# Weight blocks of a fused two-layer transformer block: units taken one after the other, matmuls of one width in runs, and unrolled gate and up bodies

## The chip, the cores and the metric

The kernel runs on one core of one Trainium2 chip. The metric is the device time of one execution in microseconds, here as the median of several runs; smaller is better. One further execution was profiled, and all rows of the trace come from it.

## What is computed

The reference takes one sequence of 256 tokens with 2048 channels through two transformer blocks in float32 (shapes and names cut to what matters here):

```
first_block:   h = norm(x); x += nsa_attention(h) @ w_out          # kv, q, cv, misc, vb, wo
               h = norm(x); x += relu(h @ ffn_w1)**2 @ ffn_w2      # ff0..ff3, fd0..fd3 (8192 hidden)
               h = norm(x); x += sigmoid(h @ ple_w_gate) * (p @ ple_w_proj)   # proj, gate
               x = norm_final(x)
second_block:  h = norm(x); m = swa_sink_attention(h) @ w_out      # k2, v2, q2, wo2
               x += norm(m)
               h = norm(x); u = conv3(h @ ffn_w_up)                # up0..up2 (5632 gates, 5632 values)
               x += norm((silu(u_gate) * u_value) @ ffn_w_down)    # dn0..dn2
```

Nearly all of the work is the product of a weight matrix with 256 columns of activations.

## The kernel before

**Layout.** Activations are kept transposed: a tile is 128 channels by 256 tokens. Each activation operand (A for the inputs of projections, H for hidden tiles) is held as a hi part, rounded to fp32r, and a lo part, the rest, side by side: `A[:, k, :, :]` is 512 columns, hi then lo. A weight block is 128 x 128. Its product with a tile is made of hi x hi, hi x lo (one matmul of 512 columns with the hi weights, line 370) and lo x hi (one matmul of 256 columns with the lo weights, line 367). The two halves of the 512-column PSUM bank are added later.

**Weights.** The host lays all weights out as a stream of 757 pieces of 512 KB, each of 8 blocks (BLK). A ring of 4 slots (SLOTS) holds them. For each piece SyncE issues the DMA (line 319), when the lo half of the piece four before it is done; ACT casts it to the hi half (`split_hi`, line 1101), when TensorE has used the slot; DVE subtracts to get the lo half (`split_lo`, line 655); TensorE waits for `lo_ready`, multiplies, and raises `piece_used` after the last matmul of the piece.

**Units and stages.** A unit is one 128-row output tile, that is K blocks (K = 16, in dn2 12, in proj 2) summed in one of four PSUM banks. A stage is a run of units with the same operand: kv, q, wo, each ff and fd, gate, q2, wo2, dn0 and dn1 have 16 units (32 pieces), k2 has 4, up0 and up1 have 32 (64 pieces), up2 has 24 (48), dn2 has 16 of 12 blocks (24). They go through `units` (line 339), called in loops of four units (`Fori`) with eight pieces each. cv, v2 and vb use other code (`compress`, `natural`, lines 498 and 394): 512-column matmuls with activations as the stationary operand, in cv in turn with runs of eight 256-column ones (line 506). proj uses the `narrow` branch of `units` (lines 359 to 361): three 256-column matmuls for each block.

**The order of the blocks** is `order` (line 104), for the host's stream and for TensorE alike. Where K is over 8 and at most 16, four units go together: blocks k = 0..3 of each of the four, then k = 4..7 of each, then the rest of each:

```python
return [(j, k) for g in range(0, n, 4) for a, b in ((0, 4), (4, 8), (8, K)) for j in range(g, g + 4) for k in range(a, b)]
```

So the four units of a group end in its last four pieces, one piece apart. Within a block the hi matmul comes first and then the lo one, in a unit's last block the other way round.

**What follows a unit.** DVE walks through the pieces in `body` (line 657). At each step it splits the piece that is LEAD + 2 = 5 ahead of the one just done, then runs `late` for the units that ended `lag` pieces ago, and then empties the bank of the units that ended in this piece: `tensor_reduce` (line 691) adds the two halves into one of four z tiles and raises `z_ready`. TensorE's next unit in the same bank waits for that (line 351). ACT's `body` (line 1108) is alike, with `each` one piece and `late` two pieces after a unit's end. POOL takes z (`take`, line 1385), mostly by a multiplication with the norm factor rs (line 1391).

In the gate stage the chain of a unit is: reduce (DVE), times rs (POOL, line 1460), sigmoid (ACT), times the proj tile and added to x (POOL, 1462 and 1464), next operand's hi and two squares (ACT, 1291 to 1293), its lo and a sum of squares (DVE, 979 to 984), another sum (POOL, 1467). In the up stages it is: reduce (DVE), times rs into ub (POOL, 1500), first tap (ACT, 1345), second and third tap (DVE, `conv`, 1046 and 1049), and for each pair of a gate and a value unit a sigmoid (ACT, 1351), two products (POOL, 1504 and 1510), a cast into H (ACT, 1354) and its lo half (POOL, 1516). up0 begins behind a norm, so its first two groups are handled by one body of eight units, in which the first four are held back four pieces (`hold`, line 1068). All these bodies are loops over groups of four units on DVE, ACT and POOL.

Of the kernel before, what the change touches and what calls it, by code (L numbers as in the profile page):

```python
# [74 lines left out]
NZ = {"cv": 0, "vb": 0, "v2": 0, "misc": 1, "proj": 0, "wo2": 0, "dn0": 0, "dn2": 0}  # L75
# [28 lines left out]
def order(n, K):  # L104

    if not 8 < K <= 16:  # L110
        return [(j, k) for j in range(n) for k in range(K)]
    return [(j, k) for g in range(0, n, 4) for a, b in ((0, 4), (4, 8), (8, K)) for j in range(g, g + 4) for k in range(a, b)]


def ends(n, K):

    at = {}
    for b, (j, k) in enumerate(order(n, K)):
        if k == K - 1:
            at.setdefault(b // BLK, []).append(j)  # L120
    return at
# [19 lines left out]
def program(nc, xT, pT, wstream, consts, setup, params, out):  # L141
# [11 lines left out]
    with ExitStack() as ctx:  # L153
# [182 lines left out]
        def _(pe):  # L336
            pe.sem_inc(piece_used, SLOTS)

            def units(p, p0, u, u0, n, K, moving, ready=None, between={}, narrow=False):

                for b, (j, k) in enumerate(order(n, K)):
                    s = (p0 + b // BLK) % SLOTS
                    if b % BLK == 0:
                        pe.wait_ge(lo_ready, p + (b // BLK + 1))
                    if k == 0:  # L350
                        pe.wait_ge(z_ready, u + (j - 3 if narrow and j >= 4 else j + 1))
                    if ready and j == 0:
                        pe.wait_ge(*ready(k))
                    bank = psum[(u0 + j) % 4 + (j // 4 % 2 * 4 if narrow else 0)]
                    w = slice(b % BLK * P, b % BLK * P + P)
                    m = moving(j, k)

                    if narrow:
                        nc.tensor.matmul(bank[:, 0:S], whi[:, s, w], m[:, 0, :], start=(k == 0), stop=False)
                        nc.tensor.matmul(bank[:, 0:S], whi[:, s, w], m[:, 1, :], start=False, stop=False)  # L360
                        last = nc.tensor.matmul(bank[:, 0:S], wlo[:, s, w], m[:, 0, :], start=False, stop=(k == K - 1))
                        if b % BLK == BLK - 1:
                            last.then_inc(piece_used, 1)
                        continue

                    def lo():
                        return nc.tensor.matmul(bank[:, 0:S], wlo[:, s, w], m[:, 0, :], start=False, stop=False)  # L367
                    if k == K - 1:
                        lo()
                    last = nc.tensor.matmul(bank[:, :], whi[:, s, w], m, start=(k == 0), stop=(k == K - 1))  # L370
                    if k < K - 1:
                        last = lo()
                    if b % BLK == BLK - 1:
                        last.then_inc(piece_used, 1)
                        if b // BLK in between:
                            between[b // BLK]()
# [112 lines left out]
            project("kv", 0, between={NORM_AT["kv"]: lambda: norm("kv")})  # L489
# [82 lines left out]
            with pe.Fori(0, 4) as it:  # L572
                units(it * 8 + PB["wo"], PB["wo"], it * 4 + UB["wo"], UB["wo"], 4, DT, lambda j, k: H[:, k, :, :],
                      lambda k: (att["nsa"]["o_ready"], k // HPG * 2 + 2))
# [7 lines left out]
            def chunk(c, first=0):  # L582
# [3 lines left out]
                with pe.Fori(0, 4) as it:  # L586
                    units(o * 64 + it * 8 + PB[fd], PB[fd], o * 32 + it * 4 + UB[fd], UB[fd], 4, CH,
                          lambda j, k: H[:, k, :, :], lambda k: (ff_ready, c * CH + (k + 1)))
            hidden(0, 0, between={NORM_AT["ff0"]: lambda: norm("ff0")})
# [5 lines left out]
            units(PB["proj"], PB["proj"], UB["proj"], UB["proj"], DT, 2, lambda j, k: pA[:, k, :, :], narrow=True)  # L595
# [11 lines left out]
            def norms_k2():  # L607
# [3 lines left out]
                  between={NORM_AT["k2"]: norms_k2})  # L611
# [7 lines left out]
            with pe.Fori(0, 4) as it:  # L619
                units(it * 8 + PB["wo2"], PB["wo2"], it * 4 + UB["wo2"], UB["wo2"], 4, DT, lambda j, k: H[:, k, :, :],  # L620
                      lambda k: (att["swa"]["o_ready"], k // HPG * 2 + 2))
# [4 lines left out]
            for c, n in enumerate(CHUNKS2):  # L626
# [5 lines left out]
                if c == 0:  # L632
                    hidden2(0, between={NORM_AT["up0"]: lambda: norm("up0", parts=(acc[:, :], acc2))})
                with pe.Fori(1 if c == 0 else 0, n // 2) as it:
                    hidden2(it)
                if n == CH:
                    with pe.Fori(0, 4) as it:
                        units(it * 8 + PB[dn], PB[dn], it * 4 + UB[dn], UB[dn], 4, n, lambda j, k: H[:, k, :, :],
                              lambda k: (up_ready, t0 + k + 1))
                else:  # L640
                    for it in range(2):
                        units(it * n + PB[dn], PB[dn], it * 8 + UB[dn], UB[dn], 8, n, lambda j, k: H[:, k, :, :],
                              lambda k: (up_ready, t0 + k + 1))
# [5 lines left out]
        def _(dve):  # L649
# [7 lines left out]
            def body(p, p0, u, u0, zu, z0, n, K, late=None, lag=1, skip=0, short=0, between={}, dst=None, narrow=False, add=False,  # L657
                     hold=0):

                at = ends(n, K)
                count = n * K // BLK
                for q in range(LEAD, count + AHEAD):
# [11 lines left out]
                    for j in at.get(q - LEAD, []):  # L679
                        dve.wait_ge(piece_used, p + (SLOTS + q - LEAD + 1))  # L680
# [959 lines left out]
```

## Time and profile before

| | us |
|---|---|
| median of 3 runs | 2458.48 (2455.64 to 2459.03) |
| the profiled execution | 2456.7 |
| its span, first to last instruction | 2454.9 |
| TensorE busy | 2312.4 (94%) |
| DVE busy | 1580.3 (64%) |
| ACT busy | 1095.4 (45%) |
| POOL busy | 768.8 (31%) |

In the trace's names PE is TensorE's matmuls, PEld its weight loads, and L691 line 691 of the kernel. A matmul's own length includes its way through the array and overlaps the next one, so the pace of TensorE is read from the distance of starts, not from lengths. PEclk is the granted TensorE clock as a share of full speed. Some matmul records can be missing, so counts of matmuls in a window are a little low. The sums of the prediction are made against the profiled execution.

### The profile page before, as it was taken

The page shows a single profiled execution, that of the slowest core. Times are in us where ns is not written, and L with a number is a line of the kernel's source. Part 1 is how long each engine was busy: PE and PEld are TensorE (multiplying, and loading weights), DVE is VectorE, ACT ScalarE, POOL GpSimd, SP SyncE. Part 2 cuts the span into 40 slices and gives each one's busy share as a digit, 9 for nine tenths or more (in the row PEclk, how much of TensorE's full clock was granted, in tenths as well). Part 3 has the DMA queues.
Part 4 walks back from the last instruction along what each step waited for, and adds up shares of the span by engine and source line. Part 5 has one row for each costly group of instructions (what it writes and reads, how often), then busy time and mean ns, then how long its engine had stood idle before and what let it go on. Part 6 is the DMA issues. An engine that isn't in the chain of part 4 may idle for free.

```text
span 2454.9 us, 39475 instructions
## 1 busy us (share of the span) xinstructions
PE 2312.4 (94%) x12668; PEld 1970.6 (80%) x12668; DVE 1580.3 (64%) x2021; ACT 1095.4 (45%) x1635; POOL 768.8 (31%) x755
## 2 busy tenths in 40 slices
PE   8999899999999999999999988978999989999996
PEld 7888668888888888888877866867788878888885
DVE  7676666666666666656666785586665566666666
ACT  5334444543443443454553354454443444434442
POOL 4111004441441441344561200244440244413443
PEclk9999899999999999999999989989999999999998
DMA  6556115555555555555545521534445544554552
GB/s 238 171 198 209 61 39 180 183 187 187 180 194 187 174 195 187 180 188 177 175 161 197 183 100 62 186 112 161 155 165 194 176 158 168 169 184 164 178 171 96
DMA packets 115118, 407.04 MB, mean 166 GB/s; under 512 B 12464, under 2 KB 16848, under 8 KB 115056
## 3 DMA queue, kind: packets, MB, share of 16 engines
q1 hardware_dynamic: 110592, 401.64, 48.4%
q10 hardware_dynamic: 4464, 4.61, 0.6%
q8 instruction: 35, 0.57, 0.1%
q14 instruction: 27, 0.22, 0.0%
HBM read 404.05 MB, written 2.15 MB: 165 GB/s over the span
## 4 chain that ended last, share of the span: by engine, by line
PE 60%; issue 20%; DVE 8%; POOL 7%; ACT 3%; POOLq 0%; DMA 0%; ACTq 0%; DVEq 0%; SPq 0%
PE bank L370 35%; PE bank L367 18%; POOL PT L1391 2%; POOL bias L1510 2%; DVE wboth L655 1%; PE bank L457 1%; PE bank L407 1%; PE bank L462 1%; PE bank L408 1%; PE bank L409 1%; POOL x L1464 1%; DVE Sm L1046 1%; ACT Sm L1156 1%; POOL Sm L1504 1%; PE bank L430 1%
## 5 line engine op out<-in xcount | busy, mean ns | idle before, releaser
L655 DVE TENSOR_TENSOR wboth<-raw,wboth 128x1024 fp32r<-128x1024 f32 x757 | 993.8, 1321 | 513.3 <-ACT wboth L1101 509.5
L370 PE MATMUL bank<-A,wboth 128*128 128x512 f32 x3200 | 1141.0, 405 | 57.8 <-DVE z L691 41.7
L1101 ACT CAST wboth<-raw 128x1024 fp32r<-128x1024 f32 x757 | 784.8, 1046 | 727.3 <-PE bank L370 325.7
L370 PE MATMUL bank<-H,wboth 128*128 128x512 f32 x2560 | 897.8, 400 | 8.8 <-DVE z L691 8.8
L367 PE MATMUL bank<-A,wboth 128*128 128x256 f32 x3200 | 876.1, 284 | 1.4 <-DVE A L735 1.4
L370 PEld LDWEIGHTS bank<-A,wboth 128*128 128x128 f32 x3200 | 599.7, 191 | 200.6 <-DVE z L691 49.5
L367 PE MATMUL bank<-H,wboth 128*128 128x256 f32 x2560 | 694.9, 282 | 0.0
L367 PEld LDWEIGHTS bank<-A,wboth 128*128 128x128 f32 x3200 | 616.2, 193 | 19.7 <-DVE A L735 1.7
L370 PEld LDWEIGHTS bank<-H,wboth 128*128 128x128 f32 x2560 | 473.4, 189 | 113.4 <-DVE z L691 10.1
L367 PEld LDWEIGHTS bank<-H,wboth 128*128 128x128 f32 x2560 | 486.6, 190 | 15.5 <-issue 0.5
L691 DVE TENSOR_REDUCE z<-bank 128x256 f32<-128x512 f32 x316 | 217.1, 687 | 55.2 <-PE bank L370 47.4
L1391 POOL TENSOR_TENSOR PT<-z,rs 128x256 f32<-128x256 f32 x88 | 131.8, 1498 | 350.2 <-DVE z L691 349.9
L1419 POOL TENSOR_TENSOR x<-x,z 128x256 f32 x80 | 79.0, 987 | 409.7 <-DVE z L691 409.7
L1391 POOL TENSOR_TENSOR bias<-z,rs 128x256 f32<-128x256 f32 x80 | 109.3, 1366 | 170.2 <-DVE z L691 170.2
L1383 POOL TENSOR_TENSOR acc<-acc,bias 128x256 f32<-128x256 f32 x80 | 79.8, 998 | 238.0 <-ACT bias L1320 152.4
L1046 DVE SCALAR_TENSOR_TENSOR Sm<-PT,par 128x256 f32<-128x256 f32 x88 | 51.5, 585 | 127.5 <-ACT PT L1345 127.5
L1345 ACT ACTIVATE PT<-PT,par 128x256 f32<-128x256 f32 x88 | 44.7, 508 | 117.7 <-POOL PT L1391 117.7
L1391 POOL TENSOR_TENSOR y<-z,Sm 128x256 f32 x32 | 37.9, 1183 | 167.0 <-DVE z L691 167.0
L1354 ACT CAST H<-bias 128x256 f32 (+1 forms) x44 | 17.9, 406 | 130.9 <-POOL bias L1510 130.9
L1259 ACT ACTIVATE Sm<-bias 128x256 f32<-128x256 f32 x64 | 26.8, 418 | 103.1 <-POOL bias L1391 103.1
L1156 ACT ACTIVATE Sm<-Sm,small 128x256 f32<-128x256 f32 (+1 forms) x128 | 56.5, 445 | 19.4 <-DVE small L761 13.1
L430 PE MATMUL bank<-kT,y 64*128 64x128 f32 (+3 forms) x256 | 51.5, 377 | 10.3 <-DVE bias L944 7.2
(196 smaller groups left out, 1394.8 us busy)
## 6 DMA issues: line engine op xcount, KB each, us to landing
raw<-wstream SPq DMA_DIRECT2D x757, 512.0 KB, 3.3
bias<-bias_rows ACTq DMA_DIRECT2D x8, 512.0 KB, 3.4
x<-xT SPq DMA_DIRECT2D x4, 512.0 KB, 6.9
out<-x SPq DMA_DIRECT2D x3, 512.0 KB, 2.7
out<-x SPq DMA_DIRECT2D x2, 256.0 KB, 2.0
Sm<-pT ACTq DMA_DIRECT2D x1, 256.0 KB, 2.7
con<-consts SPq DMA_DIRECT2D x1, 254.0 KB, 9.9
par<-params SPq DMA_DIRECT2D x1, 244.0 KB, 3.2
```

Of the source, the lines that this page charges most:

```text
L367: return nc.tensor.matmul(bank[:, 0:S], wlo[:, s, w], m[:, 0, :], start=False, stop=False)
L370: last = nc.tensor.matmul(bank[:, :], whi[:, s, w], m, start=(k == 0), stop=(k == K - 1))
L430: last = nc.tensor.matmul(bank, lhs, rhs, start=True, stop=True)
L655: V.tensor_tensor(wlo[:, s, :], raw[:, s, :], whi[:, s, :].bitcast(F32), ALU.subtract).then_inc(lo_ready, 1)
L691: V.tensor_reduce(dst(j) if dst else z[:, (z0 + j) % 4, :], psum[(u0 + j) % 4][:, :].rearrange("p (h c) -> p c h", h=2), AX, ALU.add).then ...
L1046: V.scalar_tensor_tensor(tA[:, slot, :], ub[:, slot, 1:S + 1], w[1], c0[:, slot % 2, :], ALU.mult, ALU.add).then_inc(up_step, 1)
L1101: C.copy(whi[:, s, :], raw[:, s, :]).then_inc(hi_ready, 1)
L1156: last = C.activation(probs[:, e - e0, :], probs[:, e - e0, :], ACT.Exp, bias=nmx[:, i:i + 1], accum_out=sums[:, i:i + 1])
L1383: G.tensor_tensor(dst, dst, src, ALU.add).then_inc(acc_step, 1)
L1391: return lambda zz: G.tensor_tensor(dst, zz, by, ALU.mult)
L1419: lambda zz: G.tensor_tensor(tile(x, it * 4 + j), tile(x, it * 4 + j), zz, ALU.add))
L1510: G.tensor_tensor(zr[:, j, :], tC[:, j - 1, :], tB[:, j, :], ALU.mult).then_inc(up_h, 1)
```

## The change

The order changes: all K blocks of a unit come one after the other, except in the first `mixed` groups of a stage, which keep the old order (the first group of kv, wo, ff0, each fd, gate, k2, wo2, dn0 and dn1, the first two of up0, all of dn2). In `units` a piece is done as eight hi matmuls and eight lo ones instead of eight pairs; pieces with a unit's first block begin with hi, those with its last block with lo, so that two neighbouring pieces join runs of the same width. In the gate stage each block becomes three 256-column matmuls into half a bank (`narrow`), DVE multiplies that half by rs straight into zr (`gate_in`) instead of reducing into z, and POOL's multiplication goes; the next operand of a unit is made three pieces after its end instead of two. TensorE's first iteration of wo, fd, wo2, dn0 and dn1 is written out ahead of the loop. The bodies of DVE, ACT and POOL for gate and up are written out over all units instead of looping over four; POOL's order in up and gate changes with it (below).

```diff
-def order(n, K):
...
+def order(n, K, mixed=0):
+
+    out = []
+    for g in range(0, n, 4):
+        js = range(g, min(g + 4, n))
+        cuts = ((0, 4), (4, 8), (8, K)) if g // 4 < mixed else ((0, K),)
+        out += [(j, k) for a, b in cuts for j in js for k in range(a, b)]
+    return out
...
+                    def his():
+                        for i, (j, k) in enumerate(piece):
+                            if his_first:
+                                arrive(j, k)
+                            last = nc.tensor.matmul(bank(j)[:, :], whi[:, s, cols(i)], moving(j, k), start=(k == 0), stop=(k == K - 1))
+                        return last
+
+                    def los():
+                        for i, (j, k) in enumerate(piece):
+                            if not his_first:
+                                arrive(j, k)
+                            last = nc.tensor.matmul(bank(j)[:, 0:S], wlo[:, s, cols(i)], moving(j, k)[:, 0, :], start=False, stop=False)
+                        return last
...
+                        ks = [k for _, k in piece]
+                        his_first = 0 in ks or (K - 1 not in ks and q % 2 == 1)
+                        if his_first:
+                            his()
+                            last = los()
+                        else:
+                            los()
+                            last = his()
+                    last.then_inc(piece_used, 1)
...
-                      lambda k: (a2_ready, k + 1), **more)
-            gate(0, between={NORM_AT["gate"]: lambda: norm("gate")})
+                      lambda k: (a2_ready, k + 1), narrow=True, **more)
+            gate(0, mixed=1, between={NORM_AT["gate"]: lambda: norm("gate")})
...
-                for q in range(LEAD, count + AHEAD):
+                for q in range(LEAD, count + max(AHEAD, LEAD + lag)):
...
+                        if direct:
+                            direct(j).then_inc(z_ready, 1)
+                            continue
...
+            def gate_in(j):
+
+                if j == 0:
+                    dve.wait_ge(rs_ready, 4)
+                if j >= 4:
+                    dve.wait_ge(ple_sig, j - 3)
+                return V.tensor_tensor(zr[:, j % 4, :], psum[(UB["gate"] + j) % 4][:, 0:S], rs[:, :], ALU.mult)
             dve.wait_ge(acc_zero, 3)
-            gate(0, between={NORM_AT["gate"]: lambda: norm(rs[:, :], 3).then_inc(rs_ready, 1)})
-            with dve.Fori(1, 4) as it:
-                gate(it)
+            body(PB["gate"], PB["gate"], UB["gate"], UB["gate"], ZB["gate"], ZB["gate"], DT, DT, next_lo, lag=3, mixed=1, direct=gate_in,
+                 between={NORM_AT["gate"]: lambda: norm(rs[:, :], 3).then_inc(rs_ready, 1)})
...
+                def hidden2(**more):
+                    body(PB[up], PB[up], UB[up], UB[up], ZB[up], ZB[up], 2 * n, DT, lambda j: conv(2 * t0 + j, j % 4), **more)
...
+            body(PB["gate"], PB["gate"], 0, DT, DT, sigmoid, next_input, lag=3, mixed=1,
+                 between={NORM_AT["gate"]: lambda: root(3, rs[:, :])})
...
-            with pool.Fori(0, 4) as it:
-                for j in range(4):
-                    t = it * 4 + j
-                    take(it * 4 + UB["gate"], ZB["gate"], j, mul(zr[:, j, :], rs[:, :]))
+            for t in range(DT + 2):
+                if t < DT:
                     pool.wait_ge(ple_sig, t + 1)
...
+                for i in range(n):
+                    preact(2 * i)
+                    if i:
+                        product_lo(i - 1)
+                    preact(2 * i + 1)
+                    gated(i)
+                    product(i)
+                product_lo(n - 1)
```

POOL's order for two pairs of units in up was: preact 0, preact 1, gated 0, preact 2, product 1, preact 3, product_lo 1, gated 2, product 3, product_lo 3.

## Rows read from the trace of the kernel before

**Rows 1.** Page: span, and busy time of each engine.

```profile
span 2454.9 us, 39475 instructions
PE 2312.4 (94%) x12668; PEld 1970.6 (80%) x12668; DVE 1580.3 (64%) x2021; ACT 1095.4 (45%) x1635; POOL 768.8 (31%) x755
```

**Rows 2.** Windows at stage borders: us, length, busy (count) by engine, clock, DMA.

```profile
533.40:984.60 451.20, 451.20 (x2561) 392.29 (x2560) 279.44 (x241) 192.79 (x228) 132.91 (x149) 1.00 0.55 186
1177.90:1279.30 101.40, 94.61 (x515) 81.25 (x515) 64.37 (x81) 54.17 (x91) 59.74 (x58) 0.97 0.49 165
1279.30:1333.90 54.60, 48.87 (x232) 40.53 (x231) 35.41 (x45) 23.21 (x31) 18.21 (x16) 0.94 0.46 156
1667.10:1822.30 155.20, 141.68 (x769) 121.41 (x768) 99.14 (x124) 70.07 (x100) 70.44 (x62) 0.96 0.48 164
1822.30:1916.80 94.50, 91.92 (x513) 79.69 (x513) 54.72 (x56) 35.98 (x38) 7.76 (x7) 0.98 0.55 182
1916.80:2116.00 199.20, 186.26 (x1026) 160.50 (x1025) 124.37 (x153) 88.66 (x123) 82.77 (x73) 0.97 0.49 166
2210.90:2359.00 148.10, 139.29 (x769) 119.97 (x768) 92.93 (x113) 66.28 (x91) 60.83 (x54) 0.98 0.49 167
```

**Rows 3.** Waits: who waited for whom, total us, times, longest.

```profile
PE bank L370 <- DVE z L691: 50.5, 26, 2.9
```

**Rows 4.** Timeline, end of up1: start us, length, engine, line, what.

```profile
2112.76 0.68 DVE L691 TENSOR_REDUCE z<-bank 128x256 f32<-128x512 f32 x1
...
2113.52 1.66 POOL L1391 TENSOR_TENSOR PT<-z,rs 128x256 f32<-128x256 f32 x1 [2.63 <-DVE z L691]
...
2115.32 0.51 ACT L1345 ACTIVATE PT<-PT,par 128x256 f32<-128x256 f32 x1 [2.03 <-POOL PT L1391]
...
2115.98 0.48 DVE L1046 SCALAR_TENSOR_TENSOR Sm<-PT,par 128x256 f32<-128x256 f32 x1 [1.41 <-ACT PT L1345]
...
2117.02 0.68 DVE L691 TENSOR_REDUCE z<-bank 128x256 f32<-128x512 f32 x1
...
2122.26 0.69 DVE L691 TENSOR_REDUCE z<-bank 128x256 f32<-128x512 f32 x1
```

**Rows 5.** Windows: 3 us behind the wait in dn1.

```profile
2124.00:2127.00 3.00, 3.00 (x11) 2.52 (x10) 1.46 (x4) 1.44 (x2) 2.05 (x3) 0.50 0.50 175
```

**Rows 6.** Timeline in ff3: the first and tenth 512-column matmul.

```profile
1007.00 0.40 PE L370 MATMUL bank<-A,wboth 128*128 128x512 f32 x1
...
1010.18 0.40 PE L370 MATMUL bank<-A,wboth 128*128 128x512 f32 x1
```

**Rows 7.** Timeline in wo: the first and 21st 512-column matmul.

```profile
353.02 0.40 PE L370 MATMUL bank<-H,wboth 128*128 128x512 f32 x1
...
359.96 0.40 PE L370 MATMUL bank<-H,wboth 128*128 128x512 f32 x1
```

**Rows 8.** Timeline in v2: the first and 55th 512-column matmul.

```profile
1317.62 0.39 PE L408 MATMUL bank<-wboth,H 128*128 128x512 f32 x1
...
1329.87 0.39 PE L408 MATMUL bank<-wboth,H 128*128 128x512 f32 x1
```

**Rows 9.** Timeline in proj: the first and 47th 256-column matmul.

```profile
984.64 0.28 PE L359 MATMUL bank<-pA,wboth 128*128 128x256 f32 x1
...
990.16 0.29 PE L360 MATMUL bank<-pA,wboth 128*128 128x256 f32 x1
```

**Rows 10.** Timeline in cv: the starts of two periods.

```profile
205.63 0.40 PE L407 MATMUL bank<-wboth,A 128*128 128x512 f32 x1
...
209.33 0.40 PE L407 MATMUL bank<-wboth,A 128*128 128x512 f32 x1
```

**Rows 11.** Groups by line, splits: busy us, mean ns | idle before.

```profile
L655 DVE TENSOR_TENSOR wboth<-raw,wboth 128x1024 fp32r<-128x1024 f32 x757 | 993.8, 1321 | 513.3 <-ACT wboth L1101 509.5
...
L1101 ACT CAST wboth<-raw 128x1024 fp32r<-128x1024 f32 x757 | 784.8, 1046 | 727.3 <-PE bank L370 325.7
```

**Rows 12.** Groups by line: weight loads of the lo matmuls.

```profile
L367 PEld LDWEIGHTS bank<-A,wboth 128*128 128x128 f32 x3200 | 616.2, 193 | 19.7 <-DVE A L735 1.7
```

More of the change, by code:

```diff
@@ L73 @@
 PB, UB, ZB = {}, {}, {}
-NZ = {"cv": 0, "vb": 0, "v2": 0, "misc": 1, "proj": 0, "wo2": 0, "dn0": 0, "dn2": 0}
+NZ = {"gate": 0, "cv": 0, "vb": 0, "v2": 0, "misc": 1, "proj": 0, "wo2": 0, "dn0": 0, "dn2": 0}
 _p = _u = _z = 0
@@ L101, with ends @@
                     ("g3", DT), ("conv", 3 * 2 * FF2_T), ("pos_k", CL), ("pos_v", CL), ("sink", SWA_HEADS)])
-def order(n, K):
[L110 to L115, printed above, removed]
+def order(n, K, mixed=0):
[5 more added lines that the diff above has]
+    return out
+def ends(n, K, mixed=0):
     at = {}
-    for b, (j, k) in enumerate(order(n, K)):
+    for b, (j, k) in enumerate(order(n, K, mixed)):
         if k == K - 1:
@@ L337, in _ @@
             pe.sem_inc(piece_used, SLOTS)
[L339 to L356, printed above, removed]
-                    if narrow:
[L359 to L376, printed above, removed]
@@ new lines, in units, with bank, arrive, cols @@
+            def units(p, p0, u, u0, n, K, moving, ready=None, between={}, narrow=False, banks=4, mixed=0):
+                blocks = order(n, K, mixed)
+                for q in range(len(blocks) // BLK):
+                    piece = blocks[q * BLK:q * BLK + BLK]
+                    s = (p0 + q) % SLOTS
+                    pe.wait_ge(lo_ready, p + (q + 1))
+                    def bank(j):
+                        return psum[(u0 + j) % 4 + (j // 4 % 2 * 4 if banks == 8 else 0)]
+                    def arrive(j, k):
+                        if k == 0:
+                            pe.wait_ge(z_ready, u + (j - 3 if banks == 8 and j >= 4 else j + 1))
+                        if ready and j == 0:
+                            pe.wait_ge(*ready(k))
+                    def cols(i):
+                        return slice(i * P, i * P + P)
+                    def his():
[10 more added lines that the diff above has]
+                        return last
+                    if narrow:
+                        for i, (j, k) in enumerate(piece):
+                            arrive(j, k)
+                            m = moving(j, k)
+                            nc.tensor.matmul(bank(j)[:, 0:S], whi[:, s, cols(i)], m[:, 0, :], start=(k == 0), stop=False)
+                            nc.tensor.matmul(bank(j)[:, 0:S], whi[:, s, cols(i)], m[:, 1, :], start=False, stop=False)
+                            last = nc.tensor.matmul(bank(j)[:, 0:S], wlo[:, s, cols(i)], m[:, 0, :], start=False, stop=(k == K - 1))
+                    else:
[4 more added lines that the diff above has]
+                            last = los()
+                        else:
+                            los()
+                            last = his()
+                    last.then_inc(piece_used, 1)
+                    if q in between:
+                        between[q]()
@@ L1120, in body @@
                         between[q - LEAD - 1]()
-                    for step, lag in ((late, 2), (each, 1)):
+                    for step, behind in ((late, lag), (each, 1)):
                         if step:
-                            for j in at.get(q - LEAD - lag - hold, []):
+                            for j in at.get(q - LEAD - behind - hold, []):
                                 if hold == 0 or j < 4:
                                     step(j)
-                            for j in at.get(q - LEAD - lag, []):
+                            for j in at.get(q - LEAD - behind, []):
                                 if hold and j >= 4:
```

268 lines of the change are left out of this document (135 added, 133 removed).

## The prediction

> **What bounds the kernel now.** I read the engine shares first: TensorE is busy for 94% of the 2454.9 us span, no other engine for more than 64% [rows 1]. So the question is what the remaining waits of TensorE are, and how fast it goes where it does not wait. The windows cut at the stage borders (where the matmuls of TensorE turn from operand A to operand H and back) answer both [rows 2]. From fd0 to fd2 there are 5 x 32 = 160 pieces of eight weight blocks in 451.2 us, with TensorE busy all the time: 2.82 us a piece, TensorE-bound. In up1 the same work, 64 pieces, takes 199.2 us instead of 180.5; the last 48 pieces of up0 take 155.2 and the 48 of up2 148.1 instead of 135.4; dn0 94.5, gate 101.4 instead of 90.2. The waits name the cause: 26 waits of the 512-column matmul, 50.5 us, for the DVE reduce that empties a bank [rows 3]. There is one near each border of a group of four units, in up, dn, gate and k2 alone.
>
> Why the reduce is late is seen in the timeline at the end of up1 [rows 4]. Reduce (0.68), POOL's scaling (1.66), ACT's tap (0.51), two convolution steps on DVE, and only then the next reduce, 4.26 us after the first; the last one comes 5.24 us later, because ACT first waited for POOL's product. The old order ends the four units of a group one piece (2.82 us) apart, and DVE handles a unit's convolution one piece after its end, ahead of the next reduce. So DVE falls behind by 1.4 us or more with each unit of the burst, and the bank of the fourth is empty too late. After the longer waits the clock costs extra: in the 3 us behind such a wait at the start of dn1 the granted clock is half [rows 5], 1.2 GHz instead of 2.4.
>
> **The width of the matmuls.** A block is a 512-column matmul with the hi weights and a 256-column one with the lo weights, and the old order alternates them. Nine such pairs in steady state take 3.18 us, 353.3 ns each [rows 6]. Twenty pairs just after the wait at wo take 6.94 us, 347.0 ns [rows 7]; this lasts some four pieces after a wait, then 353 returns. The trace also has runs of one width: 54 steps of 512 columns in v2 take 12.25 us, 226.9 ns each [rows 8]; 46 steps of 256 columns in proj take 5.52 us, 120.0 ns each [rows 9], directly behind 450 us of the 353 pace. Together 346.9: a run of each width costs 6.4 ns a block less than the alternation.
>
> [...]
>
> **The change, part by part.** *Runs of one width* (units). A piece becomes 8 x 226.9 + 8 x 120.0 = 2.775 us. A change of width remains once in two pieces each way; cv has such a period, 12 of 512 and 8 of 256 columns in 3.70 us [rows 10], against 12 x 0.2269 + 8 x 0.120 = 3.683, so 0.017 for both changes and 2.784 a piece. I take 2.78. The bounds are 2.775 and the old 2.82. Of the 720 pieces with pairs, gate's 32 leave. 416 lie in quiet stages (kv, q, wo, ff, fd, q2, wo2); about 16 of these already run at the quick pace, so 400 x 0.040 = 16.0 us.
>
> *Units in sequence.* Units now end two pieces (5.56 us) apart; only the first group of a stage whose operand is still being made keeps the old order. A bank is wanted again six pieces after its unit ends. At the full pace up1 would take 64 x 2.78 = 177.9 (21.3 less), up2 133.4 (14.7 less), the 48 pieces of up0 133.4 (21.8 less), dn0 89.0 (5.5 less; dn1 and dn2 repeat its waits, so 16.5 for three). That is 74.3 us. What stays: DVE per unit needs the chain of 4.26, in which one split of a piece fits, and a second split of 1.22 to 1.32 [rows 4, 11], so 5.48 to 5.58 against 5.56 of TensorE. It just fits. A lag does not stop TensorE at once: a slot freed by piece p takes 1.05 for ACT's cast and 1.3 for DVE [rows 11], and is wanted 3 x 2.78 = 8.3 us later, a slack of 6.0 us. I leave 5 us in up0, whose first eight units still come in bursts and hand on a backlog, 1.5 at the start of each dn and 2.5 for the cycle: 12 us, bounds 0 and 39 (second rival). So 62.3 us.
>
> *Gate.* Three runs of 256 columns are 24 x 120.0 = 2.88 us a piece, 92.2 for 32, dearer than 2.78. DVE's multiply out of the half bank replaces its reduce and POOL's scaling. No row has this multiply; it reads half the columns of the reduce (0.68), so I bound it by 0 and 0.68, take no cost, and DVE's per-unit work stays under the 5.76 us of two pieces. The multiply adds a wait on DVE, for the norm and from unit 4 on for ACT's sigmoid of the unit four before; behind it DVE has the next split, and TensorE waits for that. The norm was ahead of the reduce before, and that unit ended eight pieces ago, so 0. ACT's next input and DVE's lo of it move one piece back; for the last unit they stand behind a split that needs k2's first piece used, 2.8 us late, and k2 wants them in its fifth piece, 11 us on: 0. With the waits gone and 1 us left for the norm: 101.4 - 93.2 = 8.2 us.
>
> *k2 and v2* take 54.6 us [rows 2]. TensorE's norm sums wait there for POOL's additions and v2 for the norm chain. Gate's last unit no longer queues behind three others, so I take off 4 us (bounds 0 and 8: the second is about what exceeds 16 pieces).
>
> *Unrolled bodies* of DVE, ACT and POOL: the arithmetic per unit is the same, only register steps go and more code is fetched; TensorE's loops remain. Cover: the 6 us of slack above; I set 0, bounds -1 and +3. The weight DMAs are the same 757, drawn 1.5% faster at a DMA share of 0.55 in fd [rows 2], so 0. The extra TensorE bodies for first groups and the host's reordering cost nothing during the run, under the same cover. Attention, the start and the last norm are untouched.
>
> Sum: 16.0 + 62.3 + 8.2 + 4 = 90.5. The profiled execution took 2456.7 us (1.8 around its span), and the median of the runs shown is 2458.48, 1.8 above it. So 2366.2 for the former and **2368 us** for the median, 3.7% faster.
>
> **Rivals.** *First: the order of widths is not the cause.* The same alternation runs at 347.0 after a wait and 353.3 later, so something that builds up over four pieces may build up in runs too. Against it: 12 us of 512 and 5.5 us of 256 without it [rows 8, 9]. Then the 648 pieces in the sum (400, the 160 of up and the 88 of dn) keep 2.82, 25.9 us more: 2394. Chance 0.14. [...]
>
> *Second: DVE's chain paces the up bodies.* If every second unit keeps the 5.24 us step, the cycle averages 4.75 + 1.22 = 5.97, 0.41 over two pieces; over 88 units 36 us, less up to 18 for the slack of three stages: 18 to 36, say 27 more, 2395. For it: the fit within 0.1 us. Against: POOL now issues the product straight behind the convolution, so ACT's wait that made 5.24 goes. Chance 0.14.
>
> *Third, the other side: weight loads show in the run of lo matmuls.* Each 256-column matmul needs its own 128x128 load, and a load is 193 ns long in the trace [rows 12]; in the alternation each second load hides under 512 columns. In 648 pieces there are 5184 lo matmuls; the 90.5 us are gone when each takes 17 ns above 120, and at 193 the time would be 2368 + 5184 x 0.073 = 2746. The decision lies at 137 ns. Against it: proj and cv run 256 columns at 120 with as many loads as matmuls [rows 1, 9, 10]. Chance 0.03. A further 0.03 is for rivals one and two together with a cost that no row shows, which ends near no change.
>
> **How the numbers follow.** Forecast 0.66, rivals as given. The likeliest case alone spans 2351 (no residue, 2.775, 2 us more at gate and k2) to 2382. For 8 in 10 I take 2349 to 2394, up to rivals one and two, about half of which is inside. Measurement can tell about 0.2%, 5 us, from no change: faster 0.66 + 0.14 + 0.14 = 0.94, same 0.03, slower 0.03.
>
> **What would show it.** In the profile after: fd stages at 2.775 to 2.785 us a piece, with 227 and 120 ns inside a run; waits of the hi matmul for the reduce down from 26 to fewer than eight; up1 within 178 to 182 us; gate 92 to 94; no half-clock stretch in the up stages after the first 16 pieces. A pace of 2.82 in fd proves the first rival; a calm fd with up1 above 185 proves the second; lo steps above 130 ns the third. The forecast is wrong if fd does not move or if TensorE waits for weight splits in up.

## The result, and the profile after

The changed kernel takes 2362.6 us (median of four runs, 2358.8 to 2363.4) against 2457.1 for the kernel before on the same chip: a ratio of 0.9616, interval 0.9597 to 0.9635. The forecast was 2368, 3.7% faster; it is 3.8%. The profiled execution took 2362.7 us, its span 2360.8.

The page of the kernel after, span and engine busy times [rows 1]:

```profile
span 2360.8 us, 38219 instructions
PE 2265.9 (96%) x12924; PEld 1971.3 (83%) x12924; DVE 1631.3 (69%) x2021; ACT 1104.6 (47%) x1635; POOL 725.7 (31%) x739
```

The span fell by 94 us and TensorE's busy time by 46.5: so half of the gain is idle time gone, and half is busy time saved by matmuls that run faster, at the quicker pace or at full clock. The windows of the kernel after at the stage borders show where (columns as in [rows 2]; the stretches are ff2 with fd2, gate, k2 with v2, up0's last 48 pieces, dn0, up1, up2):

```profile
798.80:977.00 178.20, 178.20 (x1027) 157.45 (x1026) 117.54 (x96) 80.69 (x96) 51.75 (x64) 1.00 0.56 188
1167.70:1260.30 92.60, 92.60 (x771) 92.52 (x771) 73.40 (x85) 57.81 (x96) 50.56 (x48) 1.00 0.57 188
1260.30:1309.60 49.30, 47.06 (x231) 39.72 (x230) 34.07 (x41) 21.23 (x26) 11.37 (x10) 0.97 0.52 171
1642.30:1780.00 137.70, 134.88 (x769) 118.04 (x769) 105.80 (x130) 73.11 (x104) 71.69 (x66) 1.00 0.56 189
1780.00:1869.10 89.10, 89.10 (x514) 78.69 (x513) 51.79 (x50) 34.43 (x34) 4.82 (x4) 1.00 0.56 191
1869.10:2047.30 178.20, 178.20 (x1026) 157.48 (x1025) 144.29 (x159) 94.31 (x126) 83.37 (x76) 1.00 0.55 188
2136.40:2270.00 133.60, 133.60 (x769) 118.07 (x768) 107.65 (x118) 70.38 (x94) 62.03 (x57) 1.00 0.55 188
```

In up1 TensorE is now busy without a gap, at full clock, for the 178.2 us that 64 quiet pieces take in ff2 and fd2. Up1 became 21 us shorter: 12.9 of it were idle (199.20 less 186.26 busy), 2.3 are the new pace (64 x 0.036), and the remaining 5.8 fit the matmuls at half clock behind the waits (the mean clock of the window rose from 0.97 to 1.00).

The waits of the kernel after, TensorE's rows for the reduce (now line 716), for weight splits (685) and for A's blocks (760); line 362 is now the wide (512-column) matmul and 369 the narrow (256-column) one:

```profile
PE bank L362 <- DVE A L760: 9.1, 4, 7.8
PE bank L362 <- DVE wboth L685: 5.4, 3, 3.9
PE bank L369 <- DVE wboth L685: 4.9, 5, 1.5
PE bank L369 <- DVE A L760: 3.5, 3, 1.6
PE bank L362 <- DVE z L716: 0.3, 1, 0.3
```

The 50.5 us for reduces [rows 3] have become 0.3. Four of the waits for splits, 2.7 us together, lie in the last 48 pieces of up0; up1, dn0 and up2 have none. The timeline of TensorE in up1 shows the runs:

```profile
1894.95 3.82 PE L362 MATMUL bank<-A,wboth 128*128 128x512 f32 x16
1898.61 2.08 PE L369 MATMUL bank<-A,wboth 128*128 128x256 f32 x16
1900.52 3.82 PE L362 MATMUL bank<-A,wboth 128*128 128x512 f32 x16
```

Start to start, sixteen wide matmuls take 3.66 us (228.8 ns each) and sixteen narrow ones 1.91 (119.4 ns): 5.57 us for two pieces, 2.785 a piece. The other engines' timeline in the same place, to be read against [rows 4]:

```profile
1906.07 0.48 DVE L1086 SCALAR_TENSOR_TENSOR Sm<-PT,par,Sm 128x256 f32<-128x256 f32 x1
...
1906.63 1.65 POOL L1549 TENSOR_TENSOR bias<-Sm 128x256 f32<-128x256 f32 x1 [0.88 <-DVE Sm L1086]
...
1908.13 0.69 DVE L716 TENSOR_REDUCE z<-bank 128x256 f32<-128x512 f32 x1 [0.43 <-PE bank L362]
1908.32 0.41 ACT L1394 CAST H<-bias 128x256 fp32r<-128x256 f32 x1 [1.88 <-POOL bias L1549]
...
1913.70 0.69 DVE L716 TENSOR_REDUCE z<-bank 128x256 f32<-128x512 f32 x1 [0.23 <-PE bank L362]
```

Now DVE waits for TensorE (0.43 and 0.23 us at a reduce), not TensorE for DVE; the reduces are 5.57 us apart, two pieces. POOL's product starts 0.08 us behind the convolution (1906.07 + 0.48).

One stretch became worse. Timeline of TensorE at the start of up0 after:

```profile
1601.35 0.38 PE L369 MATMUL bank<-A,wboth 128*128 128x256 f32 x1 [1.43 <-DVE A L760]
1602.22 0.78 PE L369 MATMUL bank<-A,wboth 128*128 128x256 f32 x2 [0.49 <-DVE A L760]
1604.62 0.58 PE L369 MATMUL bank<-A,wboth 128*128 128x256 f32 x1 [1.62 <-DVE A L760]
```

The run of narrow matmuls waits for each block of A as DVE makes it, and the eight wide ones, which could have filled some of these waits, all come behind. The fifth piece takes 9.16 us, before 5.05; from wo2's last matmul to the end of the sixteenth piece it is 70.0 us, before 69.0.

### The profile page after: what moved, and what is told of

The parts are those of the page before. It is cut to its first block, busy times and chain, and to the rows that moved or that the text cites. A ratio compares the mean times of both kernels' runs of the same rounds, so it can differ in the third digit from the quotient of the medians.

```text
span 2360.8 us, 38219 instructions
## 1 busy us (share of the span) xinstructions
PE 2265.9 (96%) x12924; PEld 1971.3 (83%) x12924; DVE 1631.3 (69%) x2021; ACT 1104.6 (47%) x1635; POOL 725.7 (31%) x739
## 4 chain that ended last, share of the span: by engine, by line
PE 85%; DVE 7%; ACT 3%; POOL 3%; issue 2%; DMA 0%; POOLq 0%; SPq 0%; ACTq 0%; DVEq 0%
PE bank L362 48%; PE bank L369 25%; PE bank L376 1%; PE bank L378 1%; PE bank L377 1%; PE bank L471 1%; PE bank L476 1%; POOL bias L1431 1%; DVE wboth L685 1%; PE bank L421 1%; PE bank L423 1%; PE bank L422 1%; ACT Sm L1192 1%; DVE Sm L782 1%; ACT wboth L1141 1%
## 5 line engine op out<-in xcount | busy, mean ns | idle before, releaser
L362 PE MATMUL bank<-A,wboth 128*128 128x512 f32 x2944 | 713.2, 393 | 15.0 <-DVE A L760 9.1
L362 PEld LDWEIGHTS bank<-A,wboth 128*128 128x128 f32 x2944 | 543.4, 190 | 124.2 <-issue 15.6
L362 PE MATMUL bank<-H,wboth 128*128 128x512 f32 x2560 | 617.8, 391 | 0.3 <-DVE z L716 0.3
L362 PEld LDWEIGHTS bank<-H,wboth 128*128 128x128 f32 x2560 | 468.9, 188 | 91.3 <-issue 1.0
L369 PEld LDWEIGHTS bank<-A,wboth 128*128 128x128 f32 x2944 | 381.0, 192 | 26.7 <-DVE wboth L685 6.3
L369 PE MATMUL bank<-A,wboth 128*128 128x256 f32 x2944 | 388.0, 284 | 9.1 <-DVE wboth L685 4.9
L369 PEld LDWEIGHTS bank<-H,wboth 128*128 128x128 f32 x2560 | 331.2, 191 | 14.3
L369 PE MATMUL bank<-H,wboth 128*128 128x256 f32 x2560 | 335.8, 283 | 0.0
L1431 POOL TENSOR_TENSOR PT<-z,rs 128x256 f32<-128x256 f32 x88 | 75.0, 853 | 280.8 <-DVE z L716 280.1
L1431 POOL TENSOR_TENSOR bias<-z,rs 128x256 f32<-128x256 f32 x64 | 61.1, 955 | 160.0 <-DVE z L716 160.0
L1549 POOL TENSOR_TENSOR bias<-Sm 128x256 f32<-128x256 f32 x44 | 70.1, 1592 | 39.5 <-DVE Sm L1086 39.5
L376 PE MATMUL bank<-A,wboth 128*128 128x256 f32 x256 | 72.6, 284 | 0.0
L377 PE MATMUL bank<-A,wboth 128*128 128x256 f32 x256 | 72.4, 283 | 0.0
L378 PE MATMUL bank<-A,wboth 128*128 128x256 f32 x256 | 72.4, 283 | 0.0
L1477 POOL TENSOR_TENSOR Sm<-Sm 128x256 f32<-128x256 f32 x64 | 59.4, 927 | 33.8 <-ACT Sm L1299 33.8
```

The source lines that it names most:

```text
L362: last = nc.tensor.matmul(bank(j)[:, :], whi[:, s, cols(i)], moving(j, k), start=(k == 0), stop=(k == K - 1))
L369: last = nc.tensor.matmul(bank(j)[:, 0:S], wlo[:, s, cols(i)], moving(j, k)[:, 0, :], start=False, stop=False)
L376: nc.tensor.matmul(bank(j)[:, 0:S], whi[:, s, cols(i)], m[:, 0, :], start=(k == 0), stop=False)
L377: nc.tensor.matmul(bank(j)[:, 0:S], whi[:, s, cols(i)], m[:, 1, :], start=False, stop=False)
L378: last = nc.tensor.matmul(bank(j)[:, 0:S], wlo[:, s, cols(i)], m[:, 0, :], start=False, stop=(k == K - 1))
L1431: return lambda zz: G.tensor_tensor(dst, zz, by, ALU.mult)
```

## Experiments

After the result my theory was that of the prediction: pace by runs, waits gone by the sequence of units. The rivals were that POOL's new order or the unrolled bodies had removed the waits, and for the pace, that something other than the order of widths sets it. Every run is set against the kernel before on its chip. "Up and dn" is the time from wo2's last matmul to dn2's last in the profiled execution, one of each kernel (before 832.8 us, after 764.6).

**Pairs again**, in the changed kernel's units:

```diff
-                        if his_first:
-                            his()
-                            last = los()
...
+                        for i, (j, k) in enumerate(piece):
+                            arrive(j, k)
+                            for half in ((1, 0) if k == K - 1 else (0, 1)):
...
```

> The changed kernel with one thing undone: in every piece the eight blocks are done as pairs again, hi (512 columns) then lo (256), in a unit's last block lo then hi. Units stay in sequence, gate and the unrolled bodies stay. Theory (alternating widths is what made a piece 2.82 us): fd, ff and up1 pieces go back from 2.784 to 2.82 us, so 656 pieces x 0.036 = 24 us more, less about 5 us at the stages that start on an operand still being made, where a pair can follow each arrival: about 2381 us, up1 near 180.5. Rival (the pace came from the order of the units, or from waits that are gone): pieces stay at 2.784 and the time at 2357 to 2363 us.

2385.7 us, ratio 0.9716 (0.9700 to 0.9732): the runs are worth 23 to 25 us (by the medians, and by the ratios). The window of the same two stages, ff2 and fd2, in this kernel:

```profile
808.00:988.50 180.50, 180.50 (x1037) 157.20 (x1036) 116.52 (x97) 80.69 (x96) 52.09 (x65) 1.00 0.53 185
```

2.82 us a piece, as before: undoing the order of widths, and nothing else, brings the old pace back.

**Runs alone**: the kernel before, with the changed kernel's units and nothing else (old order of units, loops, gate).

> The kernel before with the runs of one width alone: same order of units in groups of four, same loops, same gate with 512 + 256 columns; only a piece is done as eight hi and eight lo matmuls. Theory (the two parts are independent, and the sequence is worth about 70 us by itself): quiet pieces at 2.784 to 2.79, the 26 waits for the reduce stay, up1 stays at 196 to 199 us since there DVE's burst sets the pace; 583 pieces x 0.036 = 21 us less, some 5 us given back at stage starts: 2438 to 2446 us. Rival one (runs only pay with units in sequence): 2457. Rival two (runs also relieve the bursts): under 2425.

2442.4 us, ratio 0.9951 (0.9935 to 0.9968), as expected. Its waits:

```profile
PE bank L363 <- DVE z L706: 53.7, 28, 3.3
```

In up and dn only 6.9 us are gained (825.9): a faster matmul there mostly waits longer.

**POOL's old order** in the changed kernel's unrolled up bodies:

```diff
-                for i in range(n):
+                for i in range(0, n, 2):
                     preact(2 * i)
-                    if i:
-                        product_lo(i - 1)
                     preact(2 * i + 1)
                     gated(i)
+                    preact(2 * i + 2)
                     product(i)
-                product_lo(n - 1)
+                    preact(2 * i + 3)
+                    product_lo(i)
+                    gated(i + 1)
...
```

> The changed kernel with POOL's order in the up stages as before the change (the product of a pair of units stands behind the scaling of the next unit, its lo half one scaling later still); everything else as changed. Theory (the second rival of the prediction was only averted by the new order: ACT's cast waits for that product, and behind it stand the next weight cast and tap): up1 goes from 178 to 182 to 192 us, and TensorE waits for splits or reduces there; total 2370 to 2400 us. Rival (the ring's slack of 6 us swallows it): up1 within 178 to 179.5, total 2360 to 2365.

2376.8 us, ratio 0.9678 (0.9661 to 0.9694). The total is in the range, its place is not: up1 is only 1.5 us longer, and the cost (14.0 in up and dn) lies mostly in up0 (5.1) and in the three dn (2.5 each), so the total was met by luck.

**The old order of units**, in every stage, with the new bodies:

```diff
-        cuts = ((0, 4), (4, 8), (8, K)) if g // 4 < mixed else ((0, K),)
+        cuts = ((0, 4), (4, 8), (8, K)) if 8 < K <= 16 else ((0, K),)
```

> The changed kernel with the other part undone: all groups of four units keep the old order of blocks (the host's stream and TensorE alike); runs of one width, gate's narrow blocks, the unrolled bodies and POOL's new order stay. Theory (units that end one piece apart make the reduce late, whatever runs before it): the waits for the reduce come back, over 20 of them, up1 at 195 to 199 us, dn at 91 to 92; total 2415 to 2435 us. Rival (POOL's new order and the unrolled bodies did it, the sequence only helps): up1 under 185, total under 2385.

2385.1 us, ratio 0.9716 (0.9697 to 0.9735): 30 us below my range. Only 17.8 us of reduce waits came back, and up1 took 184.1 us, not 199. So most of what I had put down to the sequence was done by the new bodies. Three more runs took these apart: POOL's order alone in the kernel before (loops, pairs, old order of units), both old orders in unrolled bodies, and before's loops of up in the changed kernel.

```diff
                     preact(0)
                     preact(1)
                     gated(0)
-                    preact(2)
                     product(1)
-                    preact(3)
+                    preact(2)
                     product_lo(1)
+                    preact(3)
                     gated(2)
```

> The kernel before, with one edit: in the loop over up's units POOL issues the product straight behind the gating and its low part one pre-activation later (the new order of POOL's queue, as far as a loop of four units allows it); order of units, pairs of widths, gate and loops are those of before. Theory (POOL's queue order is what the new bodies bring): up1 falls from 199 us to 184 to 188, as in the run with the old order of units and the new bodies (184.1), up2 from 148 to 138 to 141, and the whole to 2425 to 2437 us. Rival (it is the unrolling: no more draining of the engines' lags at the end of every loop step): up1 stays at 196 us or above and the whole at 2448 us or above.

> The changed kernel with the old order of units in every stage and, in its unrolled bodies, the old order of POOL's queue. With the earlier runs this fills the square of {order of units} by {order of POOL's queue}: new/new 2363, new/old 2377, old/new 2385. Theory (POOL's order): both old, the reduce waits come back in full, up1 194 to 199 us, whole 2405 to 2425 us. Rival (unrolling by itself): up1 184 to 187 us as with the old units alone, whole 2383 to 2395 us.

```diff
-                def hidden2(**more):
-                    body(PB[up], PB[up], UB[up], UB[up], ZB[up], ZB[up], 2 * n, DT, lambda j: conv(2 * t0 + j, j % 4), **more)
+                def hidden2(it, **more):
+                    body(it * 8 + PB[up], PB[up], it * 4 + UB[up], UB[up], it * 4 + ZB[up], ZB[up], more.pop("n", 4), DT,
+                         lambda j: conv(it * 4 + (2 * t0 + j), j % 4), **more)
...
+                with dve.Fori(2 if c == 0 else 0, n // 2) as it:
+                    hidden2(it)
...
```

> The changed kernel with the bodies of up on DVE, ACT and POOL as before: loops of four units, POOL's old order inside; the sequence of units, the runs and the gate stay. Theory (POOL's order is all that the unrolling brings, and the sequence does most of the work without it): as the run with POOL's old order alone, up1 179 to 182 us, whole 2372 to 2384 us. Rival (the drain at the end of each loop step costs too): up1 184 us or above, whole 2388 us or above.

POOL's order alone: 2417.4 us, ratio 0.9848 (0.9829 to 0.9866), up1 187.0, better than the theory. Both old: 2395.1 us (0.9756, 0.9736 to 0.9776), up1 187.1, at the edge of what the rival said and far from the theory. Loops: 2406.8 us (0.9791, 0.9770 to 0.9812), up1 188.4: the rival. Up and dn, in us:

| order of units (all with runs of one width) | loops, POOL's old order | unrolled, POOL's old order | unrolled, POOL's new order |
|---|---|---|---|
| old order of units | 825.9 | 794.6 | 787.3 |
| units in sequence | 810.0 | 778.6 | 764.6 |

Unrolling gives 31.3 and 31.4 us in the two rows (in the second the edit is the loops of up and nothing else; the kernels of the first differ in gate and in dn's first groups too), the sequence 15.9, 16.0 and 22.7, POOL's order 7.3 and 14.0. With loops and pairs POOL's order is worth more (832.8 to 793.5), so these gains replace one another in part.

Why unrolling helps can be read from two traces. Within up1 the loops and the unrolled kernel with POOL's old order execute the same list of operations on DVE, on ACT and, but for one at the window's end, on POOL. What differs is the time from the end of one operation to the start of the next one that waits for it. Timeline of DVE, ACT and POOL in up1, unrolled with POOL's old order:

```profile
2009.35 0.68 DVE L716 TENSOR_REDUCE z<-bank 128x256 f32<-128x512 f32 x1
...
2032.39 0.68 DVE L716 TENSOR_REDUCE z<-bank 128x256 f32<-128x512 f32 x1
...
2039.96 1.65 POOL L1431 TENSOR_TENSOR PT<-z,rs 128x256 f32<-128x256 f32 x1 [5.38 <-DVE z L716]
2041.64 0.51 ACT L1385 ACTIVATE PT<-PT,par 128x256 f32<-128x256 f32 x1 [2.11 <-POOL PT L1431]
2042.18 0.48 DVE L1083 SCALAR_TENSOR_TENSOR Sm<-PT,par 128x256 f32<-128x256 f32 x1 [1.18 <-ACT PT L1385]
2042.70 0.85 DVE L1086 SCALAR_TENSOR_TENSOR Sm<-PT,par,Sm 128x256 f32<-128x256 f32 x1
2043.63 1.66 POOL L1549 TENSOR_TENSOR bias<-Sm 128x256 f32<-128x256 f32 x1 [0.36 <-DVE Sm L1086]
2045.32 0.41 ACT L1394 CAST H<-bias 128x256 fp32r<-128x256 f32 x1 [2.23 <-POOL bias L1549]
```

The same in the kernel with loops, and behind it the row of its waits that has grown:

```profile
2024.45 0.68 DVE L716 TENSOR_REDUCE z<-bank 128x256 f32<-128x512 f32 x1
...
2032.24 1.65 POOL L1433 TENSOR_TENSOR PT<-z,rs 128x256 f32<-128x256 f32 x1 [5.59 <-DVE z L716]
2034.02 0.51 ACT L1386 ACTIVATE PT<-PT,par 128x256 f32<-128x256 f32 x1 [2.20 <-POOL PT L1433]
2034.68 0.88 DVE L1083 SCALAR_TENSOR_TENSOR Sm<-PT,par 128x256 f32<-128x256 f32 x1 [1.39 <-ACT PT L1386]
2035.71 0.48 DVE L1086 SCALAR_TENSOR_TENSOR Sm<-PT,par,Sm 128x256 f32<-128x256 f32 x1 [0.15 <-DVE Sm L1083]
2036.28 1.65 POOL L1551 TENSOR_TENSOR bias<-Sm 128x256 f32<-128x256 f32 x1 [0.99 <-DVE Sm L1086]
2038.06 0.41 ACT L1395 CAST H<-bias 128x256 f32 x1 [2.60 <-POOL bias L1551]
2038.47 1.05 ACT L1141 CAST wboth<-raw 128x1024 fp32r<-128x1024 f32 x1
2039.56 1.74 DVE L685 TENSOR_TENSOR wboth<-raw,wboth 128x1024 fp32r<-128x1024 f32 x1 [1.62 <-ACT wboth L1141]
...
2048.78 0.68 DVE L716 TENSOR_REDUCE z<-bank 128x256 f32<-128x512 f32 x1
```

```profile
PE bank L369 <- DVE wboth L685: 26.3, 31, 1.8
```

Take the gaps from the end of one operation to the start of the next. POOL to ACT (2041.61 to 2041.64) 0.03 us unrolled, 0.13 in the loop; ACT to DVE 0.03 and 0.15; DVE to DVE 0.04 and 0.15; DVE to POOL 0.08 and 0.09; POOL to ACT 0.03 and 0.13. So four of five hops cost 0.1 us more. They lie on a ring: reduce, scaling, tap, convolution, product, cast of H, behind which ACT has the next weight cast, behind which DVE has the next split and reduce. Once round for four units takes 24.33 us in the loop (2024.45 to 2048.78) and 23.04 unrolled (2009.35 to 2032.39); TensorE wants it every 22.3. In the loops the wait therefore shows not at the bank but at the weight split, 26.3 us.

Followed back step by step from one reduce to the one four units earlier, both rounds are the same chain of operations. Ten of its hops take 0.13 to 0.155 us in the loop and 0.03 to 0.04 unrolled, which makes 1.11 of the 1.29 us; 0.10 more is at ACT's weight cast at the end of a loop step, and 0.08 is longer operations. At each of the ten, the loop has a register step that carries the wait and stands between it and the operation. The view of these lines in up1, with the duration in ns (least, median, most):

```profile
L1386 ACTq FUSED_REGOPS  x30: 46/54/65, 1893.2 to 2070.2; - x30
L1083 DVEq FUSED_REGOPS  x30: 69/69/94, 1893.8 to 2070.8; - x30
L1086 DVEq FUSED_REGOPS  x30: 65/65/65, 1894.7 to 2071.5; - x30
L1395 ACTq FUSED_REGOPS  x14: 51/58/60, 1905.0 to 2062.3; - x14
```

The unrolled kernel has no such step on these lines. Nor is there one at the other six hops of the round (reduce to scaling, convolution to product, weight cast to split), and these are as long in either kernel, 0.08 and 0.03 us, although in the loop they too wait for a value that changes with each pass. In the program the tap, the convolution and the cast of H have an operand whose address depends on the loop counter, and the operations behind the six hops do not. What sets the ten hops apart is thus the register step behind the wait. That it makes the operand's address is read from the program; no run takes this step away and leaves the rest of the loop. That unrolling without any change of order gives the 31 us is shown.

The period of the ring, from reduce to the fourth reduce after it, repeats over nearly all of up1: 23.2 us with the old order of units in the changed kernel, 23.4 (four times 24.2) with POOL's order alone, 23.5 with both old, some 25.5 in the kernel before. In the changed kernel it is 22.27, which is TensorE's own pace.

**Pairs where an operand is awaited**, aimed at up0's fifth piece, and then, besides, the wait for the low weights put off to the narrow run:

```diff
-                    pe.wait_ge(lo_ready, p + (q + 1))
+                    hi_only = not narrow and 0 in [k for _, k in piece] and not (ready and mixed and any(j == 0 for j, _ in piece))
+                    pe.wait_ge(hi_ready if hi_only else lo_ready, p + (q + 1))
...
+                        if ready and any(j == 0 for j, _ in piece) and mixed:
+                            for i, (j, k) in enumerate(piece):
+                                arrive(j, k)
...
                             his()
+                            if hi_only:
+                                pe.wait_ge(lo_ready, p + (q + 1))
                             last = los()
```

> The changed kernel, but in the first group of the stages with mixed order, those pieces that hold blocks of the group's first unit (the only ones that wait for single operand blocks) are done as pairs. Theory (a run of lo matmuls that waits for each operand block leaves the whole run of hi matmuls for after the last arrival: up0's fifth piece took 9.16 us instead of 5.05): up0's first 16 pieces go from 70.0 to about 66 us, wo2's first piece from 87.3 to 86.4, kv loses about 1: 2355 to 2358 us. Rival (the last arrival of the operand sets the end of that piece in any case): 2362 us or, by the slower pace of pairs in some 36 pieces, 1 us more.

> The changed kernel with two edits at the starts of stages: a piece that waits for arriving operand blocks is issued in pairs again, and a piece that begins with its wide run waits for the high parts of its weights before that run and for the low parts only before the narrow run. Theory: up0's first 16 pieces about 69 us instead of 70, and the waits for the split in q, ff0, fd0 and behind up0's sixteenth piece (3 to 5 us a stage start) shrink, since eight wide matmuls of 227 ns lie between the two waits: 2352 to 2359 us, ratio to the changed kernel 0.997 to 0.999. Rival (PE waits there for the split's last member whatever the order, because the high parts come late too): 2360 to 2363 us, no difference.

First: 2360.0 us, ratio 0.9614 (0.9597 to 0.9631). Both: 2363.4 us, 0.9607 (0.9587 to 0.9628). Neither differs from the changed kernel. The first sixteen pieces take 69.0 and 68.9 us; the fifth falls from 9.16 to 6.5, but the sixth rises from 3.77 to 5.1, as it would if the blocks of A arrive no sooner. In the second run q stays at 92.6 us and ff0 and fd0 at 91.9 and 89.8, which fits the rival: the high parts come late there too.

**Gate with wide runs**: 512 and 256 columns again, and a reduce and a multiply on DVE for each unit.

> The changed kernel with gate's blocks as 512 + 256 columns in runs, as in the other stages; DVE then reduces the whole bank into zr and multiplies zr by rs in a second instruction, so it has some 1.1 us a unit instead of 0.4. Theory (narrow blocks cost TensorE 2.88 instead of 2.784 us a piece, and DVE has room for both operations in two pieces): gate 92.6 to about 89.7 us, total 3 us less, 2359 to 2360. Rival (DVE's longer work per unit makes splits or the bank late): gate at 92 us or more, total 2362 to 2366.

2359.3 us, ratio 0.9607 (0.9591 to 0.9623), no clear difference from the changed kernel. Gate takes 90.4 us, 2.2 less, but k2 and v2 take 52.2, 2.9 more, so nothing is gained there, and the total met my forecast by luck. TensorE waits in k2 for DVE's multiply of gate's last unit, which frees the bank:

```profile
PE bank L362 <- DVE bias L1026: 2.7, 1, 2.7
```

**Runs of four and of two** within a piece, one execution of each:

> The changed kernel with each piece in runs of four: four hi, four lo, four hi, four lo, or the other way round, so a run of hi follows one of lo three times in two pieces instead of once. In the trace of the changed kernel the first hi matmuls behind a run of lo are 228 to 236 ns apart and only from about the sixth at 227. Theory (a hi matmul is late for some five steps after lo ones; cost about 17 ns for each return to hi): quiet pieces at 2.80 us, total near 2373. Rival (each change of width costs the same, 2.820 being sixteen changes a piece, so 5.6 ns for both ways): 2.783 us, no change in time.

> As in runs of four, but runs of two; a run of hi follows one of lo seven times in two pieces. Theory (lateness over some five steps, which runs of two never get over): quiet pieces at 2.81 to 2.825 us, no better than the alternation; total 2380 to 2387. Rival (5.6 ns for each pair of changes): 2.795 us, total near 2369.

2376.5 and 2364.9 us; quiet pieces of 2.807 and 2.793 us. The first is nearer to my theory (a wide matmul is late for some five steps behind narrow ones), the second fits its rival (each change of width costs the same). With 2.82 for pairs and 2.785 for the joined runs of sixteen the pace doesn't follow the number of changes. Why a change of width costs time stays open.

## Why the prediction was right, and which of its steps were not

The total was right (2368 against 2362.6, inside 2349 to 2394), and so was the reading of what bounds the kernel. But one term of the sum came out by luck, with a wrong step inside it:

- *Runs of one width*: 16.0 forecast, 11.6 measured. The pace came out at 2.785, as worked out from cv (2.784) before I rounded it to 2.78 (400 x 0.036 = 14.4). The other 2.8 are mostly waits for splits that I left out, in single pieces of 3.4 to 4.4 us in q (which went from 92.0 to 92.7) and fd0, and 0.9 is the attention, which varies from one execution to the next. With both old orders q took 91.4 and fd0 89.2, against 92.7 and 89.7 after, so these waits came with the sequence. The first rival is out: the quiet stages moved, and with pairs they moved back. The Trainium skill, "TensorE: Matmul & The Clock Gate", section "Back-to-back issue gap", gives columns over 2.4 GHz plus 2.5 ns as the gap of an isolated matmul, by which one wide and one narrow would take an estimated 325 ns. These streams are slower: 228.8 + 119.4 = 348.2 in runs, and 2.82 / 8 = 352.5 in pairs.
- *Units in sequence*: 62.3 forecast, 68.2 measured in up and dn, the runs there included in both. The size holds, its cause doesn't. Sequence and runs alone would have given 22.8 (832.8 to 810.0). The failed step is "Unrolled bodies ... I set 0": unrolling is worth 31.4 on top of that, and POOL's order 14.0. I had written that only register steps go and that 6 us of slack cover them; but ten of these steps lie in each round of the ring that I had found to fit within 0.1 us, 1.1 us a round, and what comes late on a ring comes late again in each round. POOL's order I had used only as an argument against the second rival.
- The second rival, DVE's chain pacing the up bodies, didn't come about, but the run with loops is that case: a round of 24.33 us against TensorE's 22.3, up1 188.4. The fit that I gave as 5.48 to 5.58 against 5.56 holds: in the rows of the kernel after, DVE waits for TensorE by 0.2 to 0.4 us at a reduce.
- The residue of 12 us was 6.1 (74.3 less 68.2): 4.3 in up0's last 48 pieces (137.7 against 133.4), where I had left 5, and 1.0 in up0's first sixteen, which became worse and which I had left out. One of my signs of a wrong forecast did appear, in small: TensorE waits 2.7 us for weight splits in up0. The clock stays at full in up behind them, as forecast.
- *Gate*: 8.8 against 8.2, 2.894 us a piece with its waits gone. *k2 and v2*: 5.3 against 4. The third rival is out: narrow steps are 119.4 ns, not 137.

Runs, up with dn, gate, and k2 with v2 make 11.6 + 68.2 + 8.8 + 5.3 = 93.9 of the 94.0 between the two profiled executions.

## What to carry to other kernels

Where several in-order engines pass a unit round in a ring that just fits the bottleneck's period, cost every hop of it: a register step between a wait and its operation, or one instruction queued ahead of the one that the ring needs next, is paid in each round, although none of the engines of the ring looks busy. An experiment that puts back one part alone is worth more than an explanation that fits the total: here the sequence looked like the whole cause and was worth 16 to 23 us of the 68, by what else had been changed. Group matmuls by width where the operands are there; where they are still arriving, a run of one kind waits for each block, with nothing to fill the wait, though putting pairs back there gained nothing here that could be told from the scatter.

## What the runs showed of the hardware

- A hop between engines, or from one DVE operation to a dependent one, took 0.03 to 0.04 us in the unrolled up bodies (POOL to ACT, ACT to DVE, DVE to DVE). In the loops it took 0.13 to 0.155 where a register step of some 0.06 us stands between the wait and the operation. Hops without that step were as long in either: 0.03 from ACT's weight cast to DVE's split, 0.08 from DVE to POOL.
- The pace of a piece of eight wide and eight narrow matmuls is 2.82 us in pairs, 2.793 in runs of two, 2.807 in runs of four and 2.785 in runs of sixteen (quiet stages; the two windows of ff2 and fd2 shown here are at full clock).
- The first piece of wo2, which holds the attention, took between 84.2 and 92.4 us in the profiled executions of these kernels, none of which changes the attention. That is most of the scatter between the profiled executions, so a single execution of a kernel here tells no better than some 5 us.
